# Mixer and expert kernel on one core: a third pair of experts kept on the chip, and its results reloaded one turn sooner

## The chip, the cores and the metric

The kernel runs on one core of one Trainium2 chip. The metric is the time of one execution on the device in microseconds; of several runs the median is given. A core has TensorE (PE, matmul), VectorE (DVE), ScalarE (ACT), GpSimd (POOL) and SyncE (SP); SP issues most of the transfers here, and 16 DMA engines carry them.

## The reference

One decoder layer on 512 tokens of width 1024: a mixer with four gated branches, then a mixture of experts, then a final norm. The change lies in the expert part and in what follows it:

```python
for e in range(N_EXPERTS):            # 32 experts, width 256, two of them chosen for each token
    hid = jax.nn.silu(t @ w_expert_gate[e]) * (t @ w_expert_up[e])
    out = out + combine[:, e:e + 1] * (hid @ w_expert_down[e])
...
x = x + out                           # residual
return rms_norm(x, final_norm_g)
```

## The kernel before

**Turns.** The experts are taken in pairs, 16 pairs with up to 64 tokens for each expert, and one more turn (number 7) for the tokens that did not fit into the fullest expert. That makes 17 turns, 0 to 16; `LAST` is 16. In each turn (`expert_pass`) TensorE multiplies the gathered tokens by the gate and up weights (64 matmuls into bank 2, line 1904), transposes the gathered tokens of the next turn (line 1877), ScalarE makes `act_g` (962), VectorE `hid` (1008, called through `stt`), TensorE transposes it (1922), ScalarE copies it to `hidT` (964), and TensorE makes the down products in two halves of 512 columns, `b` = 0 and 1 (line 1943, banks 5 and 6, eight matmuls each).

**Weights.** A unit is one expert's gate, up or down matrix, 1 MB. SP loads the units in order into a ring of 20 slots (`load_unit_no`, issue at line 457), each as soon as the unit 20 places earlier is used up (`wait_reuse`). The two down units of turn 16 (`last_down`) are loaded last, in four halves of 512 KB (line 552); the first two raise `d_half`.

**Results.** In turns 0 to 14 the two halves are copied to `ye` (ACT line 980, DVE 1461), and GpSimd scatters the rows to `y_dram` (667): two rows for each token. The results of the last two turns, 15 and 16 (`KEPT = 2`), are not scattered. They are multiplied by their combine weight and split into a high and a low part, `yeh` (ACT, 971) and `yel` (DVE, 1008). A one-hot matrix `pick[k]` (token number against slot) brings them to the tokens by a matmul: `kept_products(k, t, ...)` makes four matmuls (two halves, two parts, line 1861) for pair `k` and tile `t` of 128 tokens.

**The end.** When all scatters have landed, SP reloads the results (`load_results`, line 540): eight loads of 512 KB into `yt[0..3]`, which lie in ring slots 1 to 4 (`ring_z`, `ring_x`, `ring_x`, `ring_y`). VectorE combines them with the residual (`gather_results`, two operations for each tile). The combined tile meets the kept products in one of two ways: for tiles 0 and 1 TensorE adds it in PSUM with an identity matmul in fp32 (`add_sum`, four matmuls, line 1869), for tiles 2 and 3 VectorE adds it (`added`, 1526). The totals of the four tiles stand in pairs of PSUM banks (`TOTALS`). Then follow the square with its sum (ACT 998), the root (ACT 1000), the reciprocal (DVE 1517), the scaling by norm and gain (`scaled`, DVE 1008) and the output store (SP 570), tile by tile in the order `NORMED`; `SUMMED` is the order of the kept products.

```python
for s in range(2):
    sp_e.wait_ge(scattered[s], 16 * (NPAIR // 2 - s))
load_results()
for w in last_down:
    wait_reuse(0, w)
```

## Time and profile before

| | |
|---|---|
| time, median of 3 runs | 751.41 us (750.5 to 754.78) |
| the profiled execution's own time | 750.8 us |
| its span, first to last instruction | 748.6 us |
| TensorE busy | 700.6 us (94%) |
| VectorE, ScalarE, GpSimd busy | 341.9, 245.6, 88.7 us |
| HBM traffic | 158.31 MB read, 15.99 MB written |
| mean granted TensorE clock | 0.974 |

The span is the time between the first and the last instruction of the profiled execution; its own time holds 2.2 us more. Busy shares are means over stages with different limits, so they don't say what a stage waits for.

### The profile page before, as it was taken

The numbers are of one execution on the slowest core, as the hardware profiler recorded it, in microseconds if no ns is written. First come the engines' busy times: TensorE is split into PE (matmuls) and PEld (weight loads), VectorE is DVE, ScalarE is ACT, GpSimd is POOL, SyncE is SP. The second block draws the span as 40 slices with busy tenths as digits, with TensorE's granted clock in tenths as the row PEclk, the third lists the DMA queues.
The fourth block names the chain that finished last, engine by engine and source line by source line (L and its number), as shares of the span: only waits on it lengthen the run. The fifth ranks groups of instructions, "written<-read, shape, count | busy, mean of one in ns | idle before, by whom it ended". The sixth has DMA issues, their size and how long they took to land.

```text
span 748.6 us, 9617 instructions
## 1 busy us (share of the span) xinstructions
PE 700.6 (94%) x3863; PEld 512.2 (68%) x3863; DVE 341.9 (46%) x635; ACT 245.6 (33%) x397; POOL 88.7 (12%) x135
## 2 busy tenths in 40 slices
PE   5999999999999999989999999699999999977875
PEld 4888988877777777768888888566555565544443
DVE  5388995255556566545546215624211212120246
ACT  7222226466656566452234211200111111010104
POOL 3002902001010101000002000201111121211000
PEclk9999999999999999999999999689999999998998
DMA  7422333422222110284305699479999999999982
GB/s 237 159 92 79 114 80 126 155 98 71 71 71 70 66 44 34 87 283 136 126 17 224 262 370 346 159 307 414 417 420 420 420 423 418 419 420 421 395 318 115
DMA packets 61582, 166.58 MB, mean 223 GB/s; under 512 B 8084, under 2 KB 39905, under 8 KB 49116
## 3 DMA queue, kind: packets, MB, share of 16 engines
q1 hardware_dynamic: 55900, 153.86, 53.7%
q0 software_dynamic: 5632, 12.05, 4.3%
q8 instruction: 32, 0.52, 0.3%
q14 instruction: 18, 0.15, 0.1%
HBM read 158.31 MB, written 15.99 MB: 233 GB/s over the span
## 4 chain that ended last, share of the span: by engine, by line
PE 81%; DMA 10%; DVE 3%; ACT 2%; SPq 2%; issue 1%; POOLq 0%; ACTq 0%; DVEq 0%
PE psum L1545 27%; PE psum L1904 13%; PE psum L1641 12%; PE psum L1943 7%; PE psum L1816 6%; DMA ring_y<-in_w_expert_up 4%; PE psum L1653 3%; DMA ring_e<-in_w_expert_down 2%; DMA raw<-in_w_gate 2%; PE psum L1692 2%; DMA y_dram<-ye,slots 1%; PE psum L1720 1%; PE psum L1775 1%; PE psum L1666 1%; PE psum L1922 1%
## 5 line engine op out<-in xcount | busy, mean ns | idle before, releaser
L1545 PE MATMUL psum<-xh,wh 128*128 128x512 f32 x256 | 100.7, 393 | 4.2 <-DVE wl L1011 2.7
L1545 PE MATMUL psum<-xh,wl 128*128 128x512 f32 x256 | 100.1, 391 | 0.0
L1545 PE MATMUL psum<-xl,wh 128*128 128x512 f32 x256 | 100.1, 391 | 0.0
L1011 DVE TENSOR_TENSOR wl<-raw,wh 128x1280 fp32r<-128x1280 f32 (+4 forms) x37 | 71.8, 1946 | 49.4 <-ACT wh L761 21.3
L1008 DVE SCALAR_TENSOR_TENSOR hid<-psum,rslot,act_g 128x256 f32<-128x256 f32 x17 | 8.2, 483 | 118.0 <-ACT act_g L962 118.0
L962 ACT ACTIVATE act_g<-psum,rslot 128x256 f32<-128x256 f32 x17 | 8.1, 475 | 156.1 <-PE psum L1904 156.1
L1545 PEld LDWEIGHTS psum<-xh,wh 128*128 128x128 f32 x256 | 48.4, 189 | 14.9 <-DVE wl L1011 3.2
L1545 PEld LDWEIGHTS psum<-xl,wh 128*128 128x128 f32 x256 | 48.5, 189 | 10.0
L1545 PEld LDWEIGHTS psum<-xh,wl 128*128 128x128 f32 x256 | 48.3, 189 | 10.1
L1641 PE MATMUL psum<-xh,wh 128*128 128x512 f32 x128 | 51.9, 405 | 0.0
L1641 PE MATMUL psum<-xl,wh 128*128 128x512 f32 x128 | 51.8, 405 | 0.0
L1641 PE MATMUL psum<-xh,wl 128*128 128x512 f32 x128 | 51.6, 403 | 0.0
L1008 DVE SCALAR_TENSOR_TENSOR sg<-cu,ch,sg 128x512 f32<-128x512 f32 x60 | 48.7, 883 | 0.0
L1904 PE MATMUL psum<-ring_h,xT 128*64 128x256 f32 x224 | 38.8, 384 | 3.0 <-DMA ring_e<-in_w_expert_up 3.0
L1904 PE MATMUL psum<-ring_w,xT 128*64 128x256 f32 x224 | 38.5, 380 | 1.1 <-DMA ring_h<-in_w_expert_up 1.1
L1461 DVE COPY ye<-psum 128x512 f32<-128x512 f32 x15 | 10.4, 691 | 59.3 <-PE psum L1943 59.3
L667 POOL DMA_INDIRECT y_dram<-ye,slots x15 | 15.2, 1013 | 175.8 <-DVE ye L1461 157.9
L1904 PE MATMUL psum<-ring_e,xT 128*64 128x256 f32 x208 | 33.9, 384 | 0.0
L1904 PEld LDWEIGHTS psum<-ring_h,xT 128*64 128x64 f32 x224 | 22.6, 139 | 14.6 <-issue 6.1
L1904 PE MATMUL psum<-ring_z,xT 128*64 128x256 f32 x96 | 26.6, 415 | 4.6 <-DMA ring_y<-in_w_expert_up 4.5
L1904 PE MATMUL psum<-ring_x,xT 128*64 128x256 f32 x112 | 30.1, 423 | 0.0
L1641 PEld LDWEIGHTS psum<-xl,wh 128*128 128x128 f32 x128 | 24.1, 188 | 6.9 <-issue 2.6
(329 smaller groups left out, 1466.8 us busy)
## 6 DMA issues: line engine op xcount, KB each, us to landing
raw<-in_w_gate SPq DMA_DIRECT2D x16, 1024.0 KB, 6.3
raw<-in_w_in SPq DMA_DIRECT2D x9, 1024.0 KB, 5.8
ring_w<-in_w_expert_gate SPq DMA_DIRECT2D x7, 1024.0 KB, 21.8
ring_w<-in_w_expert_up SPq DMA_DIRECT2D x7, 1024.0 KB, 20.3
ring_h<-in_w_expert_gate SPq DMA_DIRECT2D x7, 1024.0 KB, 21.5
ring_h<-in_w_expert_up SPq DMA_DIRECT2D x7, 1024.0 KB, 23.4
ring_e<-in_w_expert_up SPq DMA_DIRECT2D x7, 1024.0 KB, 27.9
ring_h<-in_w_expert_down SPq DMA_DIRECT2D x6, 1024.0 KB, 24.2
```

The costliest lines, as they stand in the source:

```text
L667: pool.indirect_dma_start(out=y_dram[:, :], out_offset=bass.IndirectOffsetOnAxis(ap=slots[n, p], axis=0), in_=ye[n, s, :], in_offset=None, ...
L962: act.activation(act_g[:, :], bank[2][:, 0:FE], ACT.Silu, scale=rslot[:, column(c, i)]).then_inc(S["silu"], 1)
L1008: return dve.scalar_tensor_tensor(out=out_, in0=a, scalar=s, in1=b, op0=o0, op1=o1)
L1011: return dve.tensor_tensor(dst, src, hi.bitcast(F32), ALU.subtract)
L1461: dve.tensor_copy(ye[:, s, T:2 * T], bank[6][:, :]).then_inc(S["y_b"], 1)
L1545: last = nc.tensor.matmul(dst, a, b, start=start and n == 0, stop=stop and n == len(seq) - 1)
L1641: last = nc.tensor.matmul(bank[6 + n % 2][:, :], a[:, c, f], b[:, c, :], start=c == 0 and q == 0, stop=c == KC - 1 and q == 2)
L1653: last = nc.tensor.matmul(bank[5][:, :], a[:, j, f], b[g][:, j, :], start=j == 0 and q == 0, stop=j == BJ - 1 and q == 2)
L1692: nc.tensor.matmul(bank[0][:, q0:], k_s[r:r + HD, j, kt * P:(kt + 1) * P], q_s[r:r + HD, j, q0:], start=True, stop=True).then_inc(S["z_psu ...
L1816: last = nc.tensor.matmul(bank[t][:, :], x_[:, t, c, :], w_[:, b, c, :], start=c == 0 and m == 0, stop=c == KC - 1 and m == 2)
L1904: last = nc.tensor.matmul(bank[2][half, m * FE:(m + 1) * FE], xT[:, k, half], w[h][:, k, :], start=k == 0 and m == 0, stop=k == KC - 1, sk ...
L1943: last = nc.tensor.matmul(bank[5 + b][half, :], hidT[:, m, half], w_d[h][:, m, b * T:(b + 1) * T], start=m == 0, stop=m == FE // P - 1)
```

## The change

- `KEPT` is 3: turn 14 isn't scattered either. Its parts go to a new tile `y_first` (in the memory of ring slot 0), the third one-hot matrix `pick_own` lies in the memory of `tok_no`, from which it is made.
- SP waits for turn 14's gate and up products and for the scatters up to turn 13, and then issues the reload and the last down loads.
- In turn 16 TensorE makes the kept products of pairs 0 and 1 for tiles 0, 1 and 2 ahead of the gate and up products, once the low parts of turn 15 are ready; before, products of one pair were spread over the places after them.
- `add_sum(0)` stands ahead of the transposes of `hid`, `add_sum(1)` between the two halves of the last down products, `add_sum(2)` behind them. VectorE adds only tile 3.
- The last turn's `hid` transposes go to bank 2, its down products to banks 3 and 2, and `TOTALS` is laid out anew.
- VectorE combines tiles 1 and 2 ahead of the low parts of turn 16 and tile 3 behind them. `SUMMED` and `NORMED` are both (2, 0, 1, 3).

```diff
-        KEPT = 2
+        KEPT = 3
...
+        FIRST_KEPT = LAST + 1 - KEPT
...
-        TOTALS = [psum[:, 0:2, :], psum[:, 2:4, :], psum[:, 5:7, :], psum[:, 4:8:3, :]]
-        ADDED = NT // 2
-        SUMMED, NORMED = (3, 0, 2, 1), (0, 3, 1, 2)
+        TOTALS = [psum[:, 0:2, :], psum[:, 4:6, :], psum[:, 6:8, :], psum[:, 2:4, :]]
+        ADDED = NT - 1
+        SUMMED, NORMED = (2, 0, 1, 3), (2, 0, 1, 3)
+
+        def y_bank(c, i, b):
+
+            return bank[3 - b if isinstance(c, int) and i == LAST else 5 + b]
+
+        def hidden_bank(c, i):
+
+            return bank[2 if isinstance(c, int) and i == LAST else 4]
+
+        def scatters(c, s):
+
+            return len(range(s, FIRST_KEPT, 2)) + (c - 1) * (NPAIR // 2)
...
+            sp_e.wait_ge(S["gu_done"], FIRST_KEPT + 1)
             for s in range(2):
-                sp_e.wait_ge(scattered[s], 16 * (NPAIR // 2 - s))
+                sp_e.wait_ge(scattered[s], 16 * scatters(1, s))
             load_results()
...
-                    if not isinstance(c, int) or i < LAST - 1:
+                    if not isinstance(c, int) or i < FIRST_KEPT:
                         pool.wait_ge(S["y_a"], E + 1)
...
+                        high, low = kept_parts[k]
+                        if i == LAST:
+                            gather_results(1, range(1, ADDED))
                         for b in range(2):
-                            if k:
-                                gather_results(1, range(1 + 2 * b, 3 + b))
...
+                        if i == LAST:
+                            gather_results(1, range(ADDED, NT))
                         dve.sem_inc(S["y_b"], 1)
...
+            scaled(2)
+            scaled(0)
             added(3)
-            scaled(0)
+            scaled(1)
             scaled(3)
-            added(2)
-            scaled(1)
-            scaled(2)
...
+            def kept_pairs(t):
+
+                for k in range(KEPT - 1):
+                    kept_products(k, t, k == 0, False)
...
+                    if isinstance(c, int) and i == LAST:
+                        pe.wait_ge(S["pick_ready"], KEPT)
+                        pe.wait_ge(S["y_lo"], 2 * (KEPT - 1))
+                        pe.wait_ge(S["xe"], E * 2 + 2)
+                        for t in range(ADDED):
+                            kept_pairs(t)
                     w_g = [loaded(h, 0).rearrange("p (c f) -> p c f", f=FE) for h in halves]
...
                     if isinstance(c, int) and i == LAST:
-                        pe.wait_ge(S["pick_ready"], KEPT)
-                        pe.wait_ge(S["y_lo"], 2)
-                        kept_products(0, 0, True, False)
+                        add_sum(0, 0, False)
                     pe.wait_ge(S["hid_r"], E + 1)
...
-                    if isinstance(c, int) and i == LAST:
-                        kept_products(0, 1, True, False)
...
                     if isinstance(c, int) and i == LAST:
-                        kept_products(0, 3, True, False)
                         pe.wait_ge(S["d_half"], 32)
...
                         if b and isinstance(c, int) and i == LAST:
+                            add_sum(1, 0, False)
                             for h in halves:
...
             expert_pass(0)
-            add_sum(0, 0, False)
+            add_sum(2, 0, False)
             for t in SUMMED:
-                if t == 1:
-                    add_sum(t, 0, False)
-                if t == 2:
-                    kept_products(0, t, True, False)
-                kept_products(1, t, False, True).then_inc(S["c_ps"], 1)
+                if t == ADDED:
+                    kept_pairs(t)
+                kept_products(KEPT - 1, t, False, True).then_inc(S["c_ps"], 1)
```

## Rows read from the trace of the kernel before

**Rows 1.** The page's strip: GB/s moved in each of 40 equal slices.

```profile
GB/s 237 159 92 79 114 80 126 155 98 71 71 71 70 66 44 34 87 283 136 126 17 224 262 370 346 159 307 414 417 420 420 420 423 418 419 420 421 395 318 115
```

**Rows 2.** The tile `ring_e`, issues in 685 to 686 us.

```profile
L457 SPq DMA_DIRECT2D ring_e<-in_w_expert_up x1: 2145/2145/2145, 685.5 to 685.5; - x1
...
DMA to landing us min/median/max: 27.9/27.9/27.9
```

**Rows 3.** The chain that ended last: start us, us, what.

```profile
698.56 9.07 DMA y_dram<-ye,slots
...
740.21 0.95 PE psum L1861 x4
741.18 1.12 ACT ring_x L998 x2
...
742.65 0.18 DVE stat L1517
742.85 1.28 DVE ring_x L1008
...
744.24 1.28 DVE ring_x L1008
```

**Rows 4.** Windows after 707: stretch, length, busy of each engine, PEclk, DMA share, GB/s.

```profile
707.00:713.60 6.60, 3.65 (x16) 1.06 (x16) 1.67 (x3) 1.37 (x2) 0.00 (x0) 1.00 0.83 312
713.60:720.00 6.40, 6.32 (x44) 4.31 (x46) 2.57 (x2) 0.00 (x0) 0.00 (x0) 0.73 0.98 319
720.00:727.00 7.00, 5.91 (x38) 3.76 (x34) 3.83 (x4) 0.86 (x2) 0.00 (x0) 1.00 1.03 397
727.00:731.00 4.00, 2.21 (x10) 0.71 (x12) 1.78 (x3) 0.69 (x1) 0.00 (x0) 1.00 0.25 94
```

**Rows 5.** Timeline of TensorE: start us, us, operation, idle before it and releaser.

```profile
697.75 0.62 PE L1904 MATMUL psum<-ring_w,xT 128*64 128x256 f32 x3 [1.14 <-DMA ring_h<-in_w_expert_up]
...
704.50 0.38 PE L1904 MATMUL psum<-ring_h,xT 128*64 128x256 f32 x1
...
707.01 3.65 PE L1943 MATMUL psum<-ring_h,hidT 128*64 128x512 f32 x16 [0.47 <-ACT hidT L964]
...
713.68 0.66 PE L1904 MATMUL psum<-ring_h,xT 128*64 128x256 f32 x1 [3.02 <-DMA ring_e<-in_w_expert_up]
...
728.09 1.94 PE L1943 MATMUL psum<-ring_e,hidT 128*64 128x512 f32 x8 [2.10 <-DMA ring_e<-in_w_expert_down]
730.73 1.94 PE L1943 MATMUL psum<-ring_e,hidT 128*64 128x512 f32 x8 [0.70 <-DMA ring_e<-in_w_expert_down]
...
735.61 0.39 PE L1861 MATMUL psum<-yeh,pick 128*128 128x512 f32 x1
...
737.88 0.39 PE L1861 MATMUL psum<-yeh,pick 128*128 128x512 f32 x1
...
738.33 1.88 PE L1869 MATMUL psum<-ring_x,ident 128*128 128x512 f32 x4
```

**Rows 6.** Timeline of ScalarE and VectorE, the same columns.

```profile
690.93 0.47 ACT L962 ACTIVATE act_g<-psum,rslot 128x256 f32<-128x256 f32 x1 [15.21 <-PE psum L1904]
...
704.98 0.47 ACT L962 ACTIVATE act_g<-psum,rslot 128x256 f32<-128x256 f32 x1 [9.38 <-PE psum L1904]
...
705.49 0.48 DVE L1008 SCALAR_TENSOR_TENSOR hid<-psum,rslot,act_g 128x256 f32<-128x256 f32 x1 [8.06 <-ACT act_g L962]
...
711.43 0.75 DVE L1008 SCALAR_TENSOR_TENSOR yel<-psum,w_kept,yeh 128x512 fp32r<-128x512 f32 x1 [0.90 <-ACT yeh L971]
```

**Rows 7.** The page's DMA queues: packets, MB, share of 16 engines.

```profile
q0 software_dynamic: 5632, 12.05, 4.3%
```

**Rows 8.** Windows around idle stretches of TensorE, columns as in group 4.

```profile
656.90:663.80 6.90, 3.65 (x16) 1.06 (x17) 0.96 (x2) 0.65 (x2) 1.20 (x2) 1.00 1.01 419
...
676.60:681.20 4.60, 0.13 (x2) 0.01 (x1) 0.69 (x1) 0.00 (x0) 2.01 (x2) 0.81 1.01 422
...
696.60:697.80 1.20, 0.06 (x4) 0.08 (x3) 0.69 (x1) 0.00 (x0) 0.00 (x0) 1.00 1.03 430
...
713.60:717.00 3.40, 3.32 (x16) 2.17 (x18) 0.00 (x0) 0.00 (x0) 0.00 (x0) 0.50 0.98 294
```

More of the change, by code:

```diff
@@ L118, in hybrid_trunk @@
         early.close()
+        own = region()
+        pick_own = sb(own, "pick_own", [T], F32R)
+        own.close()
         tok_no = sb(main, "tok_no", [T])
@@ L150, in hybrid_trunk @@
         UNIT_E = KC * FE
+        kept_first = region()
+        y_first = sb(kept_first, "y_first", [2, D], F32R)
+        kept_first.close()
         ring_z = sb(main, "ring_z", [2, UNIT_E])
@@ L229, in hybrid_trunk @@
         kept_l = region()
-        yel = sb(kept_l, "yel", [KEPT, D], F32R)
+        yel = sb(kept_l, "yel", [2, D], F32R)
         kept_l.close()
@@ L241, in hybrid_trunk @@
         picks = region()
-        pick = [sb(picks, f"pick{k}", [T], F32R) for k in range(KEPT)]
+        pick = [sb(picks, f"pick{k}", [T], F32R) for k in range(KEPT - 1)] + [pick_own]
         picks.close()
@@ L269, in hybrid_trunk @@
         NUP = 16
+        kept_parts = [(y_first[:, 0, :], y_first[:, 1, :])] + [(yeh[:, n, :], yel[:, n, :]) for n in (1, 0)]
         yt = [raw_slots[n].rearrange("p (j n) -> p j n", j=2) for n in (1, 2, 3, 4)]
@@ L565, in _ @@
                 for s in range(2):
-                    sp_e.wait_ge(scattered[s], 16 * (NPAIR // 2 * PASSES - s))
+                    sp_e.wait_ge(scattered[s], 16 * scatters(PASSES, s))
                 load_results()
@@ L1443, in expert_pass @@
                             x_out(E + 1, b)
[L1444 to L1445 removed]
+                    if isinstance(c, int) and i >= FIRST_KEPT:
+                        k = i - FIRST_KEPT
+                        high, low = kept_parts[k]
+                        if i == LAST:
+                            gather_results(1, range(1, ADDED))
                         for b in range(2):
[L1447 to L1448 removed]
                             half = slice(b * T, (b + 1) * T)
                             dve.wait_ge(S["y_hi"], 2 * k + b + 1)
[L1451 removed]
+                            stt(low[:, half], y_bank(c, i, b)[:, :], w_kept[:, k:k + 1], high[:, half].bitcast(F32),
                                 ALU.mult, ALU.subtract).then_inc(S["y_lo"], 1)
+                        if i == LAST:
+                            gather_results(1, range(ADDED, NT))
                         dve.sem_inc(S["y_b"], 1)
@@ L1496, in _ @@
                     for s in range(2):
-                        dve.wait_ge(scattered[s], c * (NPAIR // 2 * 16) - s * 16)
+                        dve.wait_ge(scattered[s], c * (NPAIR // 2 * 16) + scatters(0, s) * 16)
                     all_slot_hits()
@@ L1859, in kept_products @@
                         pe.wait_ge(S["y_lo"], 2 * k + b + 1)
-                    for n, part in enumerate((yeh, yel)):
-                        last = nc.tensor.matmul(TOTALS[t][:, b, :], pick[k][:, t * P:(t + 1) * P], part[:, 1 - k, half],
+                    for n, part in enumerate(kept_parts[k]):
+                        last = nc.tensor.matmul(TOTALS[t][:, b, :], pick[k][:, t * P:(t + 1) * P], part[:, half],
                                                 start=start and n == 0, stop=stop and n == 1, skip_group_check=True)
                 return last
+            def kept_pairs(t):
+                for k in range(KEPT - 1):
+                    kept_products(k, t, k == 0, False)
             def add_sum(t, n, start):
@@ L1942, in expert_pass @@
                                 half = slice(h * SLOT, (h + 1) * SLOT)
-                                last = nc.tensor.matmul(bank[5 + b][half, :], hidT[:, m, half], w_d[h][:, m, b * T:(b + 1) * T],
+                                last = nc.tensor.matmul(y_bank(c, i, b)[half, :], hidT[:, m, half], w_d[h][:, m, b * T:(b + 1) * T],
                                                         start=m == 0, stop=m == FE // P - 1)
```

22 lines of the change are left out of this document (10 added, 12 removed).

## The prediction

> **What bounds the kernel now.** I read the page's strip of slices first [rows 1]: in the last third of the span the DMA engines move about 420 GB/s, slice after slice. That is the expert part, which is fed by weight loads: a pair of experts needs 6 MB, and each 1 MB unit is issued long before it lands. The unit issued at 685.49 took 27.9 us to land [rows 2], so it landed at 713.4. At 420 GB/s that is 11.7 MB in flight.
>
> The chain of waits then tells how the end hangs together [rows 3]. The scatter of turn 14 (698.56, 9.07 us) releases SP, SP issues eight reloads and four half loads of the last down weights, the last of them is in at 730.6, and from there TensorE, ScalarE and VectorE run in a row to 745.5. The span ends at 748.6, 3.1 us after the last row, which is the last output DMA. Two numbers of that chain matter below. I call B the start of the second half of the last down products: 730.73. From B to the end of the last scaling is 14.8 us.
>
> The windows show what the late reload costs the DMA side [rows 4]: after 707 the rate is 312, 319 and 397 GB/s, and in the last four microseconds only 94. Those rates times their lengths are 2.06 + 2.04 + 2.78 + 0.38 = 7.26 MB after 707. The share is 0.83 in 707 to 713.6 (some engines ran dry while the reload was issued one by one) but 0.98 in 713.6 to 720 at 319 GB/s, so there the engines were busy and slow. And it is 0.25 at the end: engines finish at different times, and the last one sets the landing. At 713.4 one engine was still at the turn-16 weights, with reload and last down loads queued behind it. So for the engine that finishes last there was no gap to close.
>
> TensorE around the last turn [rows 5]: turn 15 ends its products at 710.7, TensorE idles 3.02 us for weights, and turn 16's gate and up products start at 713.68. Kept products and transposes follow, then an idle 2.10 us for the first down halves, eight products from 728.09, 0.70 us idle, and B.
>
> **The change, part by part.**
>
> *Turn 14 no longer scatters.* The software queue moved 12.05 MB [rows 7]. 8 zero fills of 512 KB are 4.19, 1024 gathered rows of 4 KB (512 tokens, two experts each) are 4.19, so 15 scatters are 3.67 MB, 0.245 MB each. One less is 0.6 us of DMA at 420 GB/s. In its place stand two ScalarE copies and two VectorE subtractions (0.75 us each) where one copy on each engine stood. Both engines then idle for over 8 us until turn 15's `act_g` and `hid` [rows 6], so I cost it at nothing; without that cover it would be two more operations, 1.5 us. The third one-hot row of `pick` in turn 2 is one more VectorE operation of 512 columns, at most the same 0.75, and lies under the weight waits of later turns.
>
> *The reload is issued at about 690.8*, after turn 14's gate and up, whose `act_g` starts at 690.93 [rows 6]. The scatter of turn 13 is one of the two GpSimd operations between 676.6 and 681.2 [rows 8], and is in by 690.3 at the 9.1 us of a scatter [rows 3]. That moves twelve issues on SP. Behind them on SP stand only the output stores. The twelve issues may each block while the queue is full, as the 2145 ns of the last weight issue show [rows 2], but then the queue is not empty either. What lands when: the engine that finishes last has the same work as before except its share of the scatter. So the last down halves land 0.6 us sooner at best: first halves 728.1 to 727.5, second 730.6 to 730.0. Bounds: from below, all 7.0 MB after 707 at 420 GB/s with no gap and no straggler, in by 723.7. From above, the whole 4.19 MB at the 294 GB/s of the slowest stretch, 713.6 to 717.0 [rows 8], from 713.4: 14.3 us, then the first down halves (1.05 MB at 397 GB/s, 2.6 us) at 730.3 and the second at 733.0. I take 727.5 to 728.1, nearest to the rows of the same transfers.
>
> *Kept products ahead of the last gate and up.* 3 tiles x 2 pairs x 2 halves x 2 parts = 24. They wait for the last `yel` of turn 15: 711.43 + 0.75 + 0.05 = 712.2 [rows 6]. Ten spacings between 735.61 and 737.88 are 0.227 each [rows 5], so 5.45 us, to 717.7. The weights are in at 713.4, so the gate and up products now start 4.0 us later than before. Part of that comes back: TensorE's granted clock was 0.50 from 713.6 to 717.0 (the 1.2 GHz level) after the idle of 3.0 us, which cost half of 3.4 us, 1.7. It was 1.00 (2.4 GHz) through the 1.1 us idle before turn 15 [rows 8]. Now the idle is 1.5 us, nearer to the second, so I take the full clock. Turn 15's 64 products ran from 697.75 to 704.72 (last start 704.50 plus one spacing [rows 5]), 6.97 us. New end of gate and up: 724.65.
>
> *`add_sum(0)` in front of the transposes.* The four fp32 identity matmuls hold TensorE 1.88 us (738.33 to 740.21 [rows 3, 5]): 726.5. `hid` is ready at 717.7 + 8.2 = 725.9 (in turn 15 it ended 8.2 after the first product, at 705.49 + 0.48 [rows 6]), so 0.6 of it is exposed. Transposes and `hidT` up to the first down product took 1.0 in turn 15 (705.97 to 707.01 [rows 5, 6]): 727.5. That is when the first halves land, so both bounds meet here.
>
> *`add_sum(1)` between the two down halves.* First half 1.94 [rows 5], then 1.88: B = 727.5 + 3.82 = 731.35, against 730.73. The second down halves (730.0 to 730.6) are hidden below it. `add_sum(1)` needs tile 1 combined: VectorE is free at 725.9 and has two operations of 1024 columns to do, 1.28 each as in the scaling [rows 3]: 728.5, and tile 2 at 731.1. Both are in time.
>
> *After B.* Down half 1.94, then `add_sum(2)` and four kept products to the first square 2.85 (738.33 to 741.18 [rows 3, 5]): ScalarE starts at B + 4.8. Square and root take 1.47 (741.18 to 742.65 [rows 3]): B + 6.3. VectorE scales tiles 2 and 0, 1.39 each (742.85 to 744.24 [rows 3]): B + 9.1. The 8 products of tiles 0 and 1 and the 12 of tile 3 take 20 x 0.227 after B + 4.8, so tile 3's addition starts at B + 9.3 and, at 1.28 for its 1024 columns, ends at B + 10.6, its square and root at B + 12.1, its scaling (0.20 + 1.28) at B + 13.55. That is 1.2 us less than the 14.8 of before, where two tiles had an addition on VectorE and the last tile's whole group stood last on TensorE. `yel` of turn 16 no longer waits behind a tile's combination.
>
> The sum: 731.35 + 13.55 + 3.1 = 748.0. With the first halves at 728.1 in place of 727.5 it is 748.6. I take 748.2, 0.4 us under the span of 748.6. The profiled execution took 750.8 us, the median of the three runs is 751.41; I put the difference on the median: **751.0 us**, no change that can be told. A change under 0.5% (3.8 us) can't be told from none for this kernel.
>
> **Rivals.**
>
> *The reload takes bandwidth from turn 16's weights* (the case on the other side). It is issued 17 us sooner, while 9 MB of weights are in flight. If it were served beside them, they would land up to 4.19 MB / 420 GB/s = 10 us late, 723.4; the kept products cover up to 717.7. It decides from there on: at 723.4 the end moves 5.7 us, to 753.9, a time of 756.7. Against it: the units issued one after the other land in that order, 27.9 us later [rows 2]. Chance 0.07.
> The Trainium skill ("DMA: Bandwidth & Descriptors", Queues, rings and completion order) says that each DMA engine takes the descriptors of a ring in order; by that rule the reload stays behind the weights, and the end is the forecast's 748.2 and not this rival's 753.9. The same rule speaks against the change: the reload can't land sooner than the weights ahead of it, so issuing it sooner buys only the time in which a queue had run dry.
>
> *The last down weights land late*: the slow stretch of 294 GB/s covers the whole reload. B = 730.3 + 3.82 = 734.1, end 750.8, time 753.6. For it: the engines were busy and slow there [rows 4, 8]. Chance 0.14.
>
> *The clock falls all the same* after the idle before the kept products: 1.7 us, B = 733.05, end 749.7, time 752.5. Against it: another stretch with over 3 us of idle, 656.9 to 663.8, kept its clock at 1.00 [rows 8]. Chance 0.08.
>
> *It pays in full*: loads are the only bound and land by 723.7 to 727, the end moves by 3.6 to 6.9 us, to between 741.7 and 745.0, a time of 744.5 to 747.8. Against it stands the TensorE chain above, which holds B at 731.35 whatever the loads do. It would need that chain to be 3 us too long. Chance 0.05.
>
> **How the numbers follow.** Forecast 0.60, the rivals 0.34 together, 0.06 for what I don't see. The three runs of before lie between 750.5 and 754.78, so a median of few runs can move by a microsecond. The range takes in the forecast with that scatter, the late loads and the clock: 749.0 to 754.3. Faster by over 0.5%: 0.05 and a little of the rest, 0.07. Slower: the bandwidth rival, and some of the late loads and the rest, 0.11. Within: 0.82.
>
> **What would show it.** Right: reload issues from 690.8 on; DMA at 400 GB/s or more through 707 to 713; 24 kept products from 712.2 at 0.227 each; gate and up after them at a clock of 1.00; down products at about 727.5 and B near 731.4 with little or no idle for a load between; the first square 4.8 us after B; the last row under 14 us after it. Wrong: an idle for weights of turn 16 after the kept products, a low clock from 713 on, an idle of over 1 us for the down weights, or turn 15 starting at another time than 697.75.

## The result, and the profile after

The changed kernel takes 754.97 us (median of 20 runs, 751.43 to 757.02), the kernel before on the same chips 750.78 (20 runs, 747.83 to 754.78): a ratio of 1.0043, interval 1.0027 to 1.0059. The medians lie 4.2 us apart, the means 3.2 (754.42 and 751.20); the ratio goes with the means, and 3.2 us is the difference used below. It is within the 0.5% that I called no change, but the median is 0.7 us above the range. Only the ratio's interval, from many runs, tells it from 1. The profiled execution took 755.66 us with a span of 753.4; the forecast for the span was 748.2.

The page's strip after (GB/s in each slice) and its row of the software queue answer to [rows 1, 7]:

```profile
GB/s 228 166 82 88 113 78 126 155 96 71 70 71 70 70 56 15 111 277 115 139 3 223 301 369 307 163 345 410 419 420 420 420 420 419 418 422 419 418 199 114
...
q0 software_dynamic: 5488, 11.74, 4.2%
```

In the third slice from the end the rate is 418 GB/s where it was 395, and in the next 199 where it was 318: nearly the same bytes are through sooner. The queue moves 11.74 MB for 12.05. The windows after 707 (length, busy of each engine with its instructions, granted clock, DMA share, GB/s), with one of the same length over turn 15 ahead of them, answer to [rows 4]:

```profile
698.00:704.60 6.60, 5.81 (x28) 3.75 (x30) 0.00 (x0) 0.00 (x0) 0.00 (x0) 0.50 1.02 425
707.00:713.60 6.60, 6.07 (x40) 3.25 (x38) 1.68 (x3) 1.42 (x3) 0.00 (x0) 1.00 1.01 418
713.60:720.00 6.40, 4.78 (x22) 3.24 (x19) 3.98 (x4) 0.81 (x2) 0.00 (x0) 1.00 1.03 407
720.00:727.00 7.00, 7.00 (x55) 4.70 (x56) 0.00 (x0) 0.00 (x0) 0.00 (x0) 1.00 0.74 279
727.00:731.00 4.00, 4.00 (x26) 2.14 (x22) 1.18 (x2) 0.47 (x1) 0.00 (x0) 1.00 0.03 11
```

The slump to 312 and 319 GB/s is gone, and from 720 on TensorE is busy without a gap: 7.00 of 7.00 us, 4.00 of 4.00. The loads no longer set the end. The slump itself is no fixed property of the kernel before: a second execution of that kernel (`before_again`, below) moved 408 and 373 GB/s in the same two stretches, counted from the issue of the last gate or up unit:

```profile
704.51:711.11 6.60, 5.81 (x32) 2.45 (x28) 2.43 (x4) 1.76 (x4) 0.00 (x0) 1.00 1.00 408
711.11:717.51 6.40, 5.27 (x50) 4.25 (x52) 3.32 (x3) 0.47 (x1) 0.00 (x0) 1.00 1.02 373
```

The chain of waits (start, us, what) says the same; it answers to [rows 3]:

```profile
668.56 29.98 DMA ring_h<-in_w_expert_up
698.79 10.11 PE psum L1939 x64
711.00 3.65 PE psum L1974 x16
714.65 1.62 issue
716.27 5.81 PE psum L1885 x24
722.08 7.06 PE psum L1939 x64
729.13 1.91 PE psum L1898 x4
731.75 1.94 PE psum L1974 x8
733.68 1.92 PE psum L1898 x4
735.60 1.87 PE psum L1974 x8
737.47 1.91 PE psum L1898 x4
...
```

Before, the last load on this chain was that of the last down weights. Now it is the weight load of turn **15**, issued at 668.56, and everything behind it is TensorE. The timeline of TensorE (idle before and releaser in brackets) answers to [rows 5]:

```profile
698.79 1.51 PE L1939 MATMUL psum<-ring_w,xT 128*64 128x256 f32 x5 [3.69 <-DMA ring_h<-in_w_expert_up]
...
711.00 3.65 PE L1974 MATMUL psum<-ring_h,hidT 128*64 128x512 f32 x16 [0.47 <-ACT hidT L985]
716.27 1.18 PE L1885 MATMUL psum<-y_first,pick 128*128 128x512 f32 x4 [1.62 <-issue]
...
729.06 1.98 PE L1898 MATMUL psum<-ring_z,ident 128*128 128x512 f32 x4
...
731.75 1.94 PE L1974 MATMUL psum<-ring_e,hidT 128*64 128x512 f32 x8 [0.47 <-ACT hidT L985]
733.61 1.99 PE L1898 MATMUL psum<-ring_x,ident 128*128 128x512 f32 x4
735.53 1.94 PE L1974 MATMUL psum<-ring_e,hidT 128*64 128x512 f32 x8
```

B, the start of the second down half, is 735.53; no down product waits for a load. But turn 15 stands elsewhere: it starts 1.0 us later than in [rows 5], and its first five products take 1.51 us where they took 0.83 in the trace of before, since the granted clock is 0.50 (1.2 GHz) from 698.0 to 704.6, behind an idle of 3.69 us. Its `act_g` comes at 708.98, before at 704.98 [rows 6].

The timelines of ScalarE and VectorE answer to [rows 6], and show the tail:

```profile
708.98 0.47 ACT L983 ACTIVATE act_g<-psum,rslot 128x256 f32<-128x256 f32 x1 [13.15 <-PE psum L1939]
...
740.35 1.03 ACT L1020 ACTIVATE ring_x<-psum 128x1024 f32<-128x1024 f32 x1 [0.26 <-PE psum L1885]
741.27 0.19 ACT L1020 ACTIVATION_READ_ACCUMULATOR ring_x<-psum 128x1 f32 x1
741.49 0.30 ACT L1022 ACTIVATE stat<-stat,eps 128x1 f32<-128x1 f32 x1
```

```profile
715.42 0.75 DVE L1030 SCALAR_TENSOR_TENSOR yel<-psum,w_kept,yeh 128x512 fp32r<-128x512 f32 x1 [0.91 <-ACT yeh L993]
...
740.21 1.28 DVE L1030 SCALAR_TENSOR_TENSOR ring_y<-ring_y,cw 128x1024 f32<-128x1024 f32 x1
743.21 0.17 DVE L1542 RECIPROCAL stat<-stat 128x1 f32<-128x1 f32 x1 [1.71 <-ACT stat L1022]
...
749.01 1.28 DVE L1030 SCALAR_TENSOR_TENSOR ring_y<-ring_y,stat,gfin 128x1024 f32<-128x1024 f32 x1
```

The root of the first tile ends at 741.49 + 0.30 = 741.79, VectorE has nothing to do from 741.49 on, and yet its reciprocal starts at 743.21. From B to the end of the last scaling it is 14.76 us, not 13.55.

### The profile page after: what moved, and what is told of

The parts are those of the page before. It is cut to its first block, busy times and chain, and to the rows that moved or that the text cites. A ratio compares the mean times of both kernels' runs of the same rounds, so it can differ in the third digit from the quotient of the medians.

```text
span 753.4 us, 9656 instructions
## 1 busy us (share of the span) xinstructions
PE 708.5 (94%) x3883; PEld 516.8 (69%) x3883; DVE 342.0 (45%) x636; ACT 246.2 (33%) x398; POOL 87.1 (12%) x134
## 3 DMA queue, kind: packets, MB, share of 16 engines
q0 software_dynamic: 5488, 11.74, 4.2%
## 4 chain that ended last, share of the span: by engine, by line
PE 85%; DMA 6%; DVE 3%; ACT 3%; SPq 1%; issue 1%; ACTq 0%; DVEq 0%
PE psum L1569 27%; PE psum L1939 15%; PE psum L1665 12%; PE psum L1974 7%; PE psum L1840 6%; DMA ring_h<-in_w_expert_up 4%; PE psum L1677 3%; DMA raw<-in_w_gate 2%; PE psum L1716 2%; PE psum L1744 1%; PE psum L1690 1%; PE psum L1955 1%; PE psum L1885 1%; SPq L477 1%; DVE hid L1030 1%
## 5 line engine op out<-in xcount | busy, mean ns | idle before, releaser
L1939 PE MATMUL psum<-ring_w,xT 128*64 128x256 f32 x224 | 41.4, 405 | 3.7 <-DMA ring_h<-in_w_expert_up 3.7
L1939 PE MATMUL psum<-ring_e,xT 128*64 128x256 f32 x208 | 35.9, 403 | 0.0
L1939 PEld LDWEIGHTS psum<-ring_w,xT 128*64 128x64 f32 x224 | 23.7, 146 | 12.9 <-issue 7.9
L1939 PEld LDWEIGHTS psum<-ring_e,xT 128*64 128x64 f32 x208 | 21.7, 146 | 9.9 <-issue 2.8
## 6 DMA issues: line engine op xcount, KB each, us to landing
ring_w<-in_w_expert_up SPq DMA_DIRECT2D x7, 1024.0 KB, 20.2
ring_e<-in_w_expert_up SPq DMA_DIRECT2D x7, 1024.0 KB, 27.6
```

The lines of the kernel that those rows point to most:

```text
L1939: last = nc.tensor.matmul(bank[2][half, m * FE:(m + 1) * FE], xT[:, k, half], w[h][:, k, :], start=k == 0 and m == 0, stop=k == KC - 1, sk ...
```

## The experiments

Call U the issue of the last gate/up unit of turn 16 [rows 2], A the start of turn 15's `act_g`, B as above. U is tied to the load stream, A to where turn 15 fell in it, B to the end. All timed runs are in five rounds against the kernel before, whose medians beside them were 750.8 to 751.1. The table holds the profiled execution of each kernel; the first row is the trace that the prediction was read from. U itself lies anywhere between 683.00 and 689.64, further apart than any effect here. So the table compares distances from U; the times compare the kernels. The mean of U is 686.2 in the six kernels derived from before and 686.5 in the thirteen from after: whether a part of the difference arises ahead of U can't be told from so few.

| kernel | U | A | B | A-U | B-A | B-U |
|---|---|---|---|---|---|---|
| before | 685.49 | 704.98 | 730.73 | 19.49 | 25.75 | 45.24 |
| before_again | 683.00 | 705.17 | 727.82 | 22.17 | 22.65 | 44.82 |
| hold_before | 688.45 | 708.40 | 732.25 | 19.95 | 23.85 | 43.80 |
| fill_before | 686.29 | 709.77 | 730.8 | 23.48 | 21.0 | 44.5 |
| fill24_before | 688.37 | 707.39 | 732.09 | 19.02 | 24.70 | 43.72 |
| before_sums | 685.66 | 707.00 | 730.52 | 21.34 | 23.52 | 44.86 |
| after | 685.82 | 708.98 | 735.53 | 23.16 | 26.55 | 49.71 |
| after_again | 685.52 | 706.98 | 733.53 | 21.46 | 26.55 | 48.01 |
| late_reload | 686.43 | 708.71 | 735.26 | 22.28 | 26.55 | 48.83 |
| hold_after | 687.18 | 706.48 | 733.00 | 19.30 | 26.52 | 45.82 |
| tile3_between | 689.64 | 711.65 | 738.17 | 22.01 | 26.52 | 48.53 |
| fill_after | 687.80 | 711.18 | 740.48 | 23.38 | 29.30 | 52.68 |
| after_split | 686.69 | 709.09 | 734.67 | 22.40 | 25.58 | 47.98 |
| behind | 685.99 | 705.32 | 733.24 | 19.33 | 27.92 | 47.25 |
| behind_tile3 | 685.79 | 705.13 | 733.03 | 19.34 | 27.90 | 47.24 |
| none_ahead | 685.90 | 707.92 | 730.63 | 22.02 | 22.71 | 44.73 |
| none_ahead_again | 686.43 | 705.98 | 732.87 | 19.55 | 26.89 | 46.44 |
| none_ahead_late | 686.25 | 705.74 | 732.08 | 19.49 | 26.34 | 45.83 |
| none_ahead_nosum | 685.56 | 705.03 | 727.81 | 19.47 | 22.78 | 42.25 |

(fill_before runs its sixteen down products without a gap from 728.96, so its B is half of their 3.71 us later.)

**Is it the early reload?** `late_reload`: the changed kernel, reload released by turn 15's transposes in place of turn 14's products.

```diff
-            sp_e.wait_ge(S["gu_done"], FIRST_KEPT + 1)
+            sp_e.wait_ge(S["ht_ps"], LAST)
```

> The changed kernel, with the reload and the last down loads issued only once turn 15's transposes are done, about where the kernel before issued them. TensorE theory (after the change the end hangs on TensorE's chain from the end of turn 15, and the loads are in 3 to 4 us before they are needed): the loads come in about 2 us later and still in time, the time stays that of the changed kernel, 3.2 us above before, within 1 us. Load theory (the early reload slows the loads of turns 15 and 16, which starts turn 15 later): the slip of turn 15 goes away and the time falls by 2 to 4 us, to that of before. If the late reload comes out slower than the changed kernel by over 1 us, the loads do bind and the earlier issue was worth something.

Measured 754.42, ratio 1.0044 (1.0027 to 1.0061): as the changed kernel. Issuing the reload 18 us sooner (U + 5.6 against U + 23.9) neither costs nor brings anything there. The issues on SP show one reason. First and last group in `after`, then the same two in `late_reload`:

```profile
691.40 2.10 SPq L560 DMA_DIRECT2D ring_z<-y_dram  x2
...
709.15 8.30 SPq L573 DMA_DIRECT2D ring_e<-in_w_expert_down  x4
```

```profile
710.30 2.27 SPq L560 DMA_DIRECT2D ring_z<-y_dram  x2
...
716.72 3.52 SPq L573 DMA_DIRECT2D ring_e<-in_w_expert_down  x4
```

Issued early, the twelve loads hold SP for 26 us, issued late for 10. The last down load is issued by U + 31.6 in one and by U + 33.8 in the other: of 18 us, 2 are left where it matters.

The rate over U + 21.5 to U + 34.5 does move with the issue. In the six kernels derived from before the first reload is issued at U + 20.0 to 22.2. The rate is 408 to 416 GB/s in the three where it is at U + 20.0 to 20.3, 391 at 21.6, 358 at 22.0 and 315 at 22.2, the trace of the prediction. In `late_reload` it is 312 at 23.9. B-U in the six doesn't follow it: 44.86 at 408, 43.72 at 358, 45.24 at 315.

**Is it the low clock in turn 15?** `hold_before` and `hold_after`: ten unused matmuls of 128x512 into bank 3 behind the down products of turns 12 to 15 and 12 to 14.

```diff
+                    if isinstance(c, int) and 12 <= i <= 14:
+                        pe.wait_ge(S["pick_ready"], KEPT)
+                        for n in range(10):
+                            nc.tensor.matmul(bank[3][:, :], pick[0][:, 0:P], pick[0][:, :], start=True, stop=True, skip_group_check=True)
```

> The kernel before with the same ten unused matmuls behind the down products of turns 12 to 15. TensorE theory: before the change the last down loads (in at 730.6) set the end, and TensorE idles 2.8 us for them in the last turn, so a higher clock in turns 13 to 16 is absorbed: within 0.8 us of before. If the kernel before gains 2 us or more, its end hung on the clock just as well, and the difference of the two kernels needs another cause.

> The changed kernel with ten unused matmuls of 512 columns (2.2 us, into free bank 3) behind the down products of turns 12, 13 and 14, in the time in which TensorE waits for weights. TensorE theory: the granted clock stays at 1.00 through turns 13 to 15, turn 15 ends about 3 us sooner than the 714.7 of the changed kernel's profile, and since nothing behind it waits for loads, all of it reaches the end: 2 to 3 us faster than the changed kernel, about the time of before. Load theory: the loads set the end, so nothing changes beyond 0.5 us.

`hold_before` 752.24, ratio 1.0008 (0.9991 to 1.0025); `hold_after` 755.09, 1.0053 (1.0035 to 1.0071). In its profile A-U is 19.30, and the span 750.9, but that execution was the lowest of its runs. The median did not fall, where I expected 2 to 3 us. The added products are work of their own in those turns (2.3 us each), so neither run alone separates the clock well. Taken against each other, they say more: both carry the added work and a high clock (mean of the executions 0.979), and their ratios still differ by 0.0045, as much as the two kernels without it.

Every execution's clock is on record, and it says the same. In the kernel before (139 executions beside these runs) the median is 751.8 us where the mean granted clock of the whole execution was 0.972 or less and 750.2 where it was 0.977 or more. In the changed kernel (29 executions, both runs) these are 756.0 and 753.2. So the time does follow the clock, more so after the change (2.8 us against 1.6). But at the high clock 2.9 us of difference stay, and the changed kernel's clock isn't lower as a whole: 0.974 in `after_again`, 0.973 in the kernel before beside it. The low clock is at most about a third of the excess.

**How much slack had TensorE before turn 16?** `fill_before`, `fill24_before` and `fill_after`: 12, 24 and 12 unused matmuls ahead of turn 16's gate and up.

```diff
+                        for n in range(12):
+                            nc.tensor.matmul(bank[3][:, :], pick[0][:, 0:P], pick[0][:, :], start=True, stop=True, skip_group_check=True)
```

> The kernel before with twelve unused matmuls of 512 columns (2.7 us) ahead of turn 16's gate and up products, where TensorE idled 3.0 us for weights in the profile. TensorE theory (the kernel before ends with its loads in some executions and with TensorE's chain in others, so it has slack of 0 to 2.8 us): 0.5 to 2 us slower than before, clearly less than the 3.3 us that the same filler cost the changed kernel. If it costs 2.7 us or more, the kernel before has no slack and its end hangs on TensorE just as the changed kernel's.

> The kernel before with 24 unused matmuls of 512 columns (5.45 us) ahead of turn 16's gate and up products: as much TensorE work as the changed kernel puts there, and nothing else of the change. Theory so far (before, the last down loads set the end and TensorE's chain from act_g of turn 15 to the second down half has about 7 us of slack; the changed kernel has used up that slack and more): TensorE's idle for the down weights is gone, and 0 to 2 us reach the end. Rival (the slack is only the 2.8 us of the profile, 2.7 of which the smaller filler took): 2.5 us or more slower.

> The changed kernel with twelve unused matmuls of 512 columns (2.7 us) behind the kept products ahead of the last gate and up. TensorE theory: the chain is full from there on, so all 2.7 us reach the end: 5.5 to 6.5 us above before. Load theory: TensorE waits for a load later in the turn and 0 to 1 us of it reaches the end.

`fill_before` 751.35, ratio 0.9997 (0.9977 to 1.0018); `fill24_before` 752.1, 1.0003 (0.9985 to 1.0021); `fill_after` 757.8, 1.009 (1.0067 to 1.0113). In the kernel before, even 24 products (5.45 us) cost nothing that can be told (up to 1.6 us is within the interval); in the changed one 12 products (2.7 us) cost 0.0047 x 751 = 3.5 us. The down products of `fill_before`, then of `fill24_before`:

```profile
728.96 3.71 PE L1947 MATMUL psum<-ring_e,hidT 128*64 128x512 f32 x16
```

```profile
729.48 1.94 PE L1947 MATMUL psum<-ring_e,hidT 128*64 128x512 f32 x8
732.09 1.94 PE L1947 MATMUL psum<-ring_e,hidT 128*64 128x512 f32 x8 [0.67 <-DMA ring_e<-in_w_expert_down]
```

In `fill_before`, where turn 15 fell late (A-U 23.48), no half waits for a load. In `fill24_before`, where it fell early (19.02), the first half no longer waits and the second still does. The added products have eaten most of the slack or all of it, and B-U is still no larger than before.

**Kept products behind gate and up.** `behind`: the 24 kept products stand behind the gate and up products, tile 0's ahead of the transposes of `hid`, the others and `add_sum(0)` behind them.

```diff
-                        for t in range(ADDED):
-                            kept_pairs(t)
...
-                        add_sum(0, 0, False)
+                        kept_pairs(0)
...
+                    if isinstance(c, int) and i == LAST:
+                        for t in range(1, ADDED):
+                            kept_pairs(t)
+                        add_sum(0, 0, False)
```

> The changed kernel with the 24 kept products behind turn 16's gate and up products, tile 0's ahead of the transposes of hid and tiles 1 and 2 and add_sum(0) behind them. The gate and up products can then start with the end of turn 15's down products (714.7 in the changed kernel's profile, weights in at 713.4) and not at 722.1; the waits for act_g, hid and hidT are filled. TensorE theory: the second down half starts near 733.6 and not 735.6, 2.0 us faster than the changed kernel, 1.2 us above before. Load theory: no change beyond 0.5 us, since the loads are in at the same time.

Measured 754.62, ratio 1.0039 (1.002 to 1.0058), a gain of 0.3 us over the changed kernel where I expected 2.0; the intervals don't tell it from none. Its gate and up products start with their loads again, at U + 27.0:

```profile
713.00 0.40 PE L1937 MATMUL psum<-ring_h,xT 128*64 128x256 f32 x1 [2.00 <-DMA ring_e<-in_w_expert_up]
...
733.24 1.94 PE L1976 MATMUL psum<-ring_e,hidT 128*64 128x512 f32 x8
```

From there to B it is 20.2 us without a wait. So the end no longer hangs on turn 15, but the same work lies between the landing of the weights and B, and the 5.45 us stand behind the 2.00 us of idle and not in it.

**The tail.** `tile3_between`: VectorE combines tile 3 between the two low parts of turn 16, not behind them; `behind_tile3` is both edits.

```diff
+                            if b and i == LAST:
+                                gather_results(1, range(ADDED, NT))
                             dve.wait_ge(S["y_hi"], 2 * k + b + 1)
...
-                        if i == LAST:
-                            gather_results(1, range(ADDED, NT))
```

> The changed kernel with tile 3's combination between the two low parts of turn 16 on VectorE and not behind them. In the changed kernel's profile the first reciprocal starts 1.4 us after its root, with VectorE idle 1.7 us behind that combination, where the program reads the flag and branches; that idle should then lie ahead of the first root. Expected: the first reciprocal straight behind its root, tile 3's addition 1.1 us sooner, 1.1 us faster than the changed kernel (2.1 us above before). If the 1.7 us was something else (the root's semaphore, a port), nothing changes.

> Both edits: kept products behind gate and up, and tile 3's combination between the low parts. TensorE theory: 2.0 + 1.1 = 3.1 us faster than the changed kernel, within 0.7 us of before. Load theory: as the changed kernel, or 1.1 us under it.

`tile3_between` 753.24, ratio 1.0021 (1.0002 to 1.0039), 1.7 us under the changed kernel's ratio where I expected 1.1; `behind_tile3` 753.5, 1.0028 (1.0013 to 1.0043), 1.1 us where I expected 3.1. The intervals overlap with the changed kernel's, so the gain is firmer in the traces. The reciprocal and the last scaling of `tile3_between`:

```profile
744.56 0.16 DVE L1542 RECIPROCAL stat<-stat 128x1 f32<-128x1 f32 x1 [2.37 <-ACT stat L1022]
...
750.62 1.28 DVE L1030 SCALAR_TENSOR_TENSOR ring_y<-ring_y,stat,gfin 128x1024 f32<-128x1024 f32 x1
```

The root ends at 744.45, the reciprocal follows 0.11 later, and from B (738.17) to the end it is 13.73 us, 1.0 less than in the changed kernel (13.68 in `behind_tile3`, 13.73 in `after_split`, 14.76 or 14.77 in `after`, `after_again` and `behind`). VectorE's idle time is 2.37 us, but now it lies ahead of the root.

`after_split` adds that pair 0's four products of tile 0 don't wait for the low parts of turn 15.

```diff
-                        pe.wait_ge(S["y_lo"], 2 * (KEPT - 1))
+                        pe.wait_ge(S["y_lo"], 2)
                         pe.wait_ge(S["xe"], E * 2 + 2)
-                        for t in range(ADDED):
-                            kept_pairs(t)
+                        kept_products(0, 0, True, False)
+                        pe.wait_ge(S["y_lo"], 2 * (KEPT - 1))
+                        kept_products(1, 0, False, False)
+                        for t in range(1, ADDED):
+                            kept_pairs(t)
```

> The changed kernel with tile 3's combination between the low parts, and with pair 0's four products of tile 0 (turn 14's results, ready long before) ahead of the wait for the low parts of turn 15. TensorE idled 1.6 us in that wait; 0.9 of it is then filled with work that stood behind it. TensorE theory: 0.9 + 1.1 = 2.0 us faster than the changed kernel, 1.2 us (0.15%) above before. If nothing comes of it beyond the 1.0023 of tile 3's move, the chain does not start at that wait.

Measured 752.5, ratio 1.0016 (0.9998 to 1.0035), the best version with the whole change in it and where I expected it (1.0015), though it can't be told from `tile3_between` alone. The idle of 1.62 us is 0.44, and B-A 25.58:

```profile
716.34 0.50 PE L1885 MATMUL psum<-yeh,pick 128*128 128x512 f32 x1 [0.44 <-DVE yel L1030]
```

**The sums alone.** `before_sums`: the kernel before with `add_sum(0)` ahead of the wait for the first down halves, `add_sum(1)` between the halves, and VectorE combining tiles 1 to 3 ahead of the low parts.

```diff
                         kept_products(0, 3, True, False)
+                        add_sum(0, 0, False)
                         pe.wait_ge(S["d_half"], 32)
...
                         if b and isinstance(c, int) and i == LAST:
+                            add_sum(1, 0, False)
...
-                            if k:
-                                gather_results(1, range(1 + 2 * b, 3 + b))
+                            if k and b == 0:
+                                gather_results(1, range(1, NT))
...
             expert_pass(0)
-            add_sum(0, 0, False)
             for t in SUMMED:
-                if t == 1:
-                    add_sum(t, 0, False)
```

> The kernel before, with two pieces of the change alone: add_sum(0) in front of the wait for the first down halves, where TensorE idled 2.1 us, and add_sum(1) between the down halves, where it idled 0.7; and VectorE combines tiles 1 to 3 ahead of the low parts of turn 16. No third kept pair, no early reload. Theory: add_sum(0) costs nothing there and add_sum(1) delays the second half by 1.2 us; behind it 3.8 us of TensorE work are gone, and the rest is then paced by squares and scalings: 0.7 to 1.9 us faster than before. If TensorE were the bound of the kernel before, add_sum(0) ahead would gain nothing and the time would stay.

Measured 752.42, ratio 1.0018 (1.0 to 1.0036): no gain, where I expected 0.7 to 1.9 us. From B to the end of the span its profile has 16.8 us, before 17.9, and its B-U is 44.86, as before. By the profile it should have been faster; why the median is not stays open. (Its mean clock is 0.973, the kernel before beside it 0.974.)

**Work left out.** `none_ahead` leaves the 24 kept products of tiles 0 to 2 out (its sums start their totals); `none_ahead_late` has the late reload beside it; `none_ahead_nosum` leaves `add_sum(1)` out too. The changed kernel and `none_ahead` were run once more, and the kernel before as if it were a change.

```diff
-                        for t in range(ADDED):
-                            kept_pairs(t)
...
-                            add_sum(1, 0, False)
+                            add_sum(1, 0, True)
```

> The changed kernel with the 24 kept products of pairs 0 and 1 for tiles 0 to 2 left out of the work (their part of the result is missing), early reload as in the change. Theory: TensorE then has room, the end hangs on the loads again, and these are in about 42 us after the issue of the last gate or up unit, where the kernel before had the second down half at 43.7 to 45.2 us: 2 to 3 us faster than before, 5 to 6 us faster than the changed kernel. Rival (the slowest DMA engine never ran dry, so issuing sooner lands nothing sooner but the scatter's 0.6 us): 0.5 to 1 us faster than before.

> The same with the reload and last down loads issued behind turn 15's transposes, about where the kernel before issued them. Theory: the second down half stands at 44 to 45 us after the last unit's issue again, within 0.7 us of before, and 2 to 3 us slower than the early one. Rival: as the early one, within 0.7 us.

> The same, and add_sum(1) left out as well (tile 1 also lacks its combined results). The second down half then starts with its own loads: if the early reload lands them sooner, at 42 to 43.5 us after the last unit's issue and 1 to 2 us sooner than with add_sum(1) between; if it lands nothing sooner, at 44 to 45 us as in the kernel before.

> The kernel before, unchanged, for a second profile and as a null. Theory: act_g of turn 15 starts anywhere from 705 to 711 in different executions (705.0 in the first profile), the second down half at 730.5 to 732.5 whatever it does, and the time is that of before within 0.2%. If the second down half moves with turn 15's act_g, the slack is not there.

> The changed kernel once more, for a second profile. Theory (its end hangs on TensorE from turn 15 on): 26.5 us from turn 15's act_g to the second down half, as in the first profile, and 47 to 50 us from the issue of the last gate or up unit to it, against 43.7 to 45.2 in the kernel before; time 1.0043 of before within 0.2%.

> The changed kernel without the 24 kept products ahead once more (their part of the result is missing). If the last turns are the whole cause: within 0.2% of before, and the 1.0028 was spread. If a second cause lies elsewhere: 1.002 to 1.004 again, with the last turns as fast as in the kernel before.

| kernel | median us | ratio | interval |
|---|---|---|---|
| none_ahead | 752.27 | 1.0028 | 1.0007 to 1.005 |
| none_ahead_again | 752.18 | 1.0012 | 0.9997 to 1.0028 |
| none_ahead_late | 754.01 | 1.0047 | 1.0023 to 1.007 |
| none_ahead_nosum | 750.33 | 0.9992 | 0.9976 to 1.0008 |
| before_again | 751.34 | 0.9996 | 0.9977 to 1.0014 |
| after_again | 754.1 | 1.0044 | 1.0028 to 1.0059 |

I expected `none_ahead` 2 to 3 us faster than before; it is 0.9 to 2.1 us slower. Still, with the products gone, the excess over before falls from 0.0043 to between 0.0012 and 0.0028; with `add_sum(1)` gone as well, nothing is left of it. Together with `fill_after` this shows that the excess goes with TensorE work ahead of B. What is left of it in `none_ahead` goes with the clock: the mean of the executions is 0.9712, 0.9726 and 0.9707 in `none_ahead`, `none_ahead_again` and `none_ahead_late`, and 0.9737, 0.9732 and 0.9737 in the kernel before beside them, but 0.9734 against 0.9732 in `none_ahead_nosum`. The down products of `none_ahead_nosum`:

```profile
725.23 1.94 PE L1971 MATMUL psum<-ring_e,hidT 128*64 128x512 f32 x8 [1.61 <-DMA ring_e<-in_w_expert_down]
727.81 1.94 PE L1971 MATMUL psum<-ring_e,hidT 128*64 128x512 f32 x8 [0.65 <-DMA ring_e<-in_w_expert_down]
```

Both halves wait for their loads again, and B-U is 42.25, against 43.80 to 45.24 in the three traces of before's kind in which both halves wait: in this trace the loads come 1.5 to 3.0 us sooner. The median doesn't show it: 0.9992 is at best 1.8 us faster. The first halves land at U + 39.7 to 41.0 in the three traces of this group with the early reload, at U + 40.4 in the one with the late reload, and at U + 41.2 to 42.6 in before, before_again and hold_before. By these traces the gain doesn't come from the time of the issue; the third kept pair, with one scatter less, is what the four have in common, but that it is the cause is not shown. The times leave it open: `none_ahead_late` is 1.7 us slower than `none_ahead` beside it, with intervals that overlap. `none_ahead_again` shows what an idle before the down products does:

```profile
726.23 3.68 PE L1972 MATMUL psum<-ring_e,hidT 128*64 128x512 f32 x8 [3.33 <-DMA ring_e<-in_w_expert_down]
729.84 3.10 PE L1898 MATMUL psum<-ring_x,ident 128*128 128x512 f32 x4
```

The eight products take 3.68 us, where they take 1.94 elsewhere, and the sum 3.10 for 1.98: 2.9 us more. TensorE came earlier than in `none_ahead` (A-U 19.55 for 22.02) and waited longer, and its B-U is 1.7 us above that one's. Work taken out ahead of a wait can come back as a low clock behind it.

## Why the prediction was wrong

**The step that failed** is the one under "TensorE around the last turn": turn 15 was taken to start at 697.75 and end at 710.7, as in the one trace, and the idle times behind it were taken as slack of that size. With the tail below it accounts for most of the miss; the clock comparison above says that it isn't all. The prediction had named "turn 15 starting at another time than 697.75" among the signs of being wrong, but put no price on it. The table shows that A-U is 19.0 to 23.5 in nineteen executions, of both kernels alike; the trace of before, at 19.49, lies near the low end. Two things move it: turn 15 starts between U + 11.8 and U + 13.5, and its 64 products run at full clock (7.2 us to `act_g`) or partly at half (8.5 to 10.2).

In the kernel before this doesn't matter: with A-U from 19.0 to 23.5, B-U stays within 43.7 to 45.2. In before, before_again and hold_before TensorE waits 1.8 to 2.2 us for the first down weights; in the other three its added or moved work stands in that place, and B is no later for it. In the changed kernel B-A is 26.5 in five executions out of five: the chain from turn 15 to B has no wait for a load, and every late A moves B in full. The work ahead of B grew by 12 kept products net (24, where 12 of pair 0 stood, 2.7 us) and two sums (3.8 us), 6.5 us. In the trace of before the idle times and the low clock of turn 16 held 3.02 + 2.10 + 0.70 + 1.7 = 7.5 us, of which 1.62 remain; 6.5 - 5.9 = 0.6, and B-A grew by 0.8. From the mean position of turn 15 the slack is 1.5 us smaller (20.98 - 19.49), and that is gone before the last turn begins. These are traces; that this mean also sets the median is argued, not shown.

**The chain itself was right.** From A to B the prediction has 731.35 - 704.98 = 26.37 (its own terms, 727.5 + 3.82, add to 731.32); measured 26.52 to 26.55. Its parts in the profile of after: kept products at A + 7.29 (7.22 predicted), 5.81 us for the 24 (5.45), down products at A + 22.77 (22.52). The kept products had the full clock, as assumed.

**The sum.** In the profile of after, B is 4.18 us later than predicted: 0.33 from U, 0.71 from turn 15's start against U, 2.96 from its clock, 0.18 from the chain. The tail adds 1.21. Together 5.4 us: 748.0 becomes 753.4. For the median, as an estimate: the mean of A-U is 20.98, so B-U is 20.98 + 26.55 = 47.5 after, and 44.5 (mean of the six kernels derived from before) to 45.0 (before and before_again) before. B to the end of the span is 17.87 in both. The difference, 2.5 to 3.0 us, is near what the runs measured (3.2). It fits less well where the clock was high: the nine traces with turn 15 at full clock have a mean A-U of 19.44, which gives B-U 46.0 after and a difference of 1.0 to 1.5 us, and the high-clock executions differ by 2.9. The rest is open.

**The tail was mis-sized** by 1.2 us: 14.76 for 13.55. The first square starts at B + 4.8, as predicted. The term that was off is the step from "Square and root take 1.47" to "VectorE scales tiles 2 and 0": the first scaling was put at B + 6.3 and started at B + 7.9 (743.41). Square and root took 1.44, but tile 3's combination ends at 741.49 in the profile of after, and VectorE goes on 1.71 later. In the code a read of the overflow flag and a branch stand there; that they take the time is read from the code and not measured by itself. `tile3_between` moved that stretch ahead of the root and got 1.0 us back. I had counted VectorE's operations and not what stands between them. In the profiles of before, before_again and before_sums the idle at that place is 0.94 us, with TensorE named as the releaser, so there the same read was through sooner. In the changed kernel tile 3's combination ends with a wait for its own last operation, so the read comes after it; in the kernel before no such wait stands ahead of the read. That this makes the difference is an argument from the code.

**The rivals.** *Bandwidth taken from turn 16's weights*: no. The last unit lands 27.6 us after its issue with the reload issued behind it (27.9 before), and in `behind` its products start at U + 27.0. By the rule of the Trainium skill ("DMA: Bandwidth & Descriptors", Queues, rings and completion order) the reload stays behind the weights; these two numbers agree. *The last down weights land late*: no, DMA ran at 407 GB/s where 319 were before, and no down product waited. (In `late_reload` it ran at 312 again, and no down product waited either.) *The clock falls*: it did, but in turn 15 and not in turn 16; the prediction priced 1.7 us for the wrong stretch. *It pays in full*: refuted. With TensorE's work ahead of B left out (`none_ahead_nosum`) the second half starts 1.5 to 3.0 us sooner in one trace, yet the median is that of before. The forecast that the last down halves land 0.6 us sooner at best is too low by that trace, but hidden behind TensorE.

**Open**: why `before_sums` and `none_ahead_nosum` gain nothing by the median when their traces are shorter from U on, whether the lower clock is the cause of what is left of `none_ahead`'s excess (0.0012 and 0.0028 in two samples of the same kernel), and where the part of the 2.9 us at high clock comes from that the chain doesn't give. No version with the whole computation was faster than the kernel before beyond the interval.

## What to carry to other kernels

When a stage is bound by a stream of loads, its slack on the compute engine differs from one execution to the next; measure it by adding unused work in steps (here 5.45 us cost nothing that could be told), and not from one trace. The same holds for a DMA rate: 315 GB/s in one trace of the kernel before were 391 in the next. Before moving work ahead of a wait, ask what the chain hangs on once the wait is gone: if it is an event whose place varies by 4 us, reckon with its mean place and not with the one seen. A load issued sooner behind a long queue lands hardly sooner (18 us of issue were 2 us for the last down load). And in a tail, count the instructions that the profile doesn't call busy (flag reads, branches) as work of their engine.

## What was not expected of the hardware

- The same turn of the same program starts its gate and up products 11.8 to 13.5 us after the same load issue, and runs them at a granted clock of 1.00 or 0.50 in different executions. The idle ahead of turn 15 was 0.71 to 1.41 us where its first five products took 0.83, 2.42 to 2.81 where they took 0.97 to 1.22, and 2.95 to 4.66 where they took 1.51.
- An idle of 3.33 us before the down products was followed by 2.9 us lost at the lower clock, one of 4.01 us (`none_ahead_late`, half 2.65, sum 2.93) by 1.7 us, one of 2.36 us (`none_ahead`, half 1.94) by nothing.
- The stretch of 319 GB/s at a share of 0.98 in before isn't there in three other kernels derived from it (408 to 416 GB/s over the same 13 us) and is there again in `late_reload` (312). The first reload was issued at U + 20.0 to 20.3 in the fast ones and at U + 22.2 and 23.9 in the slow ones. What made the engines slow at a share near 1 is not shown.
